# Sigmoid gates of the merge in seven block products, two whole gates ahead of the attention's last transposes; the last up projection likewise

## The chip, the core and the metric

The kernel runs on one core of one Trainium2 chip. The time is device microseconds (us) for one execution of the whole program, all weights streamed from HBM in fp32. Engines are named as in the profile: PE (TensorE matmul) and PEld (its weight load), DVE (VectorE), ACT (ScalarE), POOL (GpSimd) and SP, whose queue issues all weight loads.

## The reference, cut to what matters

Two transformer blocks run one after the other. The first has two layers ("a0", "a1"). The second has two layers too ("b0", "b1"), and the change is in those. There, layer 0 works on 512 tokens (256 of x and 256 of a context), layer 1 on the 256 tokens of x alone.

```python
def merge_branches(o_mla, o_gqa, o_four, gate_cols, lp):
    g_mla, g_gqa, g_four = jnp.split(jax.nn.sigmoid(gate_cols), N_BRANCH, axis=-1)
    y = (g_mla * (o_mla @ lp["w_br_mla"])
         + g_gqa * (o_gqa @ lp["w_br_gqa"])
         + g_four * (o_four @ lp["w_four"]))
    return y @ lp["w_o"]

def conv_ffn_2(h, lp):
    u = h @ lp["w_up"]                       # 1024 -> 2 x 2816
    u = depthwise_conv_width_3(u) + lp["conv_b"]
    a, v = jnp.split(u, 2, axis=-1)
    return (jax.nn.silu(a) * v) @ lp["w_down"]
```

The gate columns are `h @ w_in[:, 1952:]`, 3 x 1024 columns with an inner length of 1024.

## The kernel before, in words

Activations stand feature-major: 128 features on the partitions, tokens along the free axis. A matmul of the program has a 128x128 weight tile as its stationary side and 256 or 512 tokens as its moving side; the trace has two MATMUL records for each. Weight tiles come in the order of use as slabs. There are two slots for slabs (`slots`), and a slab is asked for by SP as soon as the slab before the last is used up (`static_slab`, `load`).

**The merge** (stage `merge{l}`, from L2437). There are 8 output tiles m and 3 branches b, 24 steps. A step is a gate (8 matmuls, `tensor_gate`, L2455) and a branch (4 matmuls, L2471). ACT forms the sigmoid (L2484), DVE the product with the branch (L2491), POOL adds the branches up in `Y` (L2500). A slab holds the 36 tiles of one m. The first gate stands inside the attention: `tensor_pairs` calls `late` after the transposes of the last unit but one, `tensor_gate_first`.

**Seven block products.** The up projection of b0 (`SEVEN`) is done in another way. Its weights for one m, gate half and value half, are taken as a 2x2 matrix of blocks (half by inner half), and the tokens as a 2x2 matrix (inner half by token half). The product of two such matrices needs seven block products in place of eight, in the form of Winograd. A block product is 4 matmuls (`product`, L858). POOL forms the sums s1 and s3 of weight blocks, DVE s2 and s4 (L947, L949), before PE uses them, and DVE forms four token sums t1 to t4 once per projection. Afterwards DVE combines the products: u2, u3, c22, c21 (L1000 to L1010) and c12 (L991); ACT copies p1 out of PSUM (L929). Block 0 is done whole (L840), while the sums for block 1 are formed. The order on PE within a block is p1, p6, p7, p5, p4, a12 (added to p1), p3.

**The up projection of b1** is done plainly (`tensor_up`, L660): per m 16 matmuls with 256 columns, then bias and scale on ACT (L729), four convolution taps on DVE (L754), silu on ACT (L732), the product on POOL (L781). Both forms run as a loop of 4 pairs or blocks a turn, with the rest written out.

The order of work on each engine is the program's order; nothing reorders it. Waits are on counting semaphores that each engine's own instructions raise.

## Time and profile before

| | us |
|---|---|
| median of 3 runs | 2697.74 |
| lowest and highest | 2694.82 and 2699.82 |
| the profiled execution | 2699.97 |
| its span, first to last instruction | 2697.9 |
| PE busy in the span | 2626.1 |

The mean granted clock of PE in the profiled execution is 0.979 of full speed. The profile's page gives totals; the timeline gives groups of like instructions with their start and their extent. Neighbouring groups of PE overlap a little, because the drain of one matmul lies beside the next, so a group's price is the distance from its start to the next group's start.

### The profile page before, as it was taken

What the parts mean: (1) busy time and instruction counts of PE and PEld (TensorE: products, weight loads), DVE (VectorE), ACT (ScalarE), POOL (GpSimd) and SP (SyncE); (2) the same over time, 40 slices, a digit from 0 to 9 for tenths busy, and PEclk for the clock granted to TensorE, in tenths of its full rate; (3) what the DMA queues carried; (4) which work ended last, traced back from release to release, by engine and by line L of the source; (5) the groups of instructions that cost most, each with busy time, mean ns of one, the idle gap of its engine ahead of it and who ended that gap; (6) DMA issues with size and microseconds to landing.
All of it is one profiled execution on the core that took longest, in us unless ns stands there. A gap on an engine that the chain in (4) does not pass through costs nothing.

```text
span 2697.9 us, 28700 instructions
## 1 busy us (share of the span) xinstructions
PE 2626.1 (97%) x11142; PEld 1942.6 (72%) x11142; DVE 934.2 (35%) x1793; ACT 534.5 (20%) x1075; POOL 350.9 (13%) x322
## 2 busy tenths in 40 slices
PE   7999999999899999999999999999999999999999
PEld 5756888886577888744654446888846865887887
DVE  3024167741313868313620003554401235102220
ACT  1122132111212221112530001222100124102320
POOL 0011111000101111001420001233200004100100
PEclk9989999999899999999999999999999998999999
DMA  5422377733234776121001112122311220233342
GB/s 201 154 94 78 110 281 275 288 138 143 91 124 167 270 268 245 63 95 40 1 36 70 70 66 94 63 93 93 118 47 70 94 103 1 106 143 134 146 174 102
DMA packets 31394, 333.84 MB, mean 124 GB/s; under 512 B 2880, under 2 KB 9152, under 8 KB 9152
## 3 DMA queue, kind: packets, MB, share of 16 engines
q1 hardware_dynamic: 31296, 332.45, 32.7%
q8 instruction: 72, 1.18, 0.2%
q14 instruction: 26, 0.21, 0.0%
HBM read 331.39 MB, written 1.05 MB: 123 GB/s over the span
## 4 chain that ended last, share of the span: by engine, by line
PE 95%; DVE 3%; POOL 1%; ACT 1%; issue 1%; DMA 0%; DVEq 0%; POOLq 0%; ACTq 0%
PE PS L552 26%; PE PS L660 17%; PE PS L858 9%; PE PS L2455 9%; PE PS L1414 5%; PE PS L1572 5%; PE PS L2471 5%; PE PS L1232 3%; PE PS L1584 2%; PE PS L2052 2%; PE PS L1255 2%; PE PS L1243 2%; PE PS L430 1%; PE PS L2168 1%; PE PS L2324 1%; PE PS L1084 1%
## 5 line engine op out<-in xcount | busy, mean ns | idle before, releaser
L660 PE MATMUL PS<-XN,slot 128*128 128x256 f32 x2112 | 461.3, 382 | 10.0 <-DVE XN L492 5.1
L660 PEld LDWEIGHTS PS<-XN,slot 128*128 128x128 f32 x2112 | 404.4, 192 | 66.9 <-issue 11.1
L552 PE MATMUL PS<-arena,slot 128*128 128x256 f32 x1824 | 400.9, 382 | 9.7 <-POOL arena L1973 5.4
L552 PEld LDWEIGHTS PS<-arena,slot 128*128 128x128 f32 x1824 | 349.5, 192 | 60.2 <-POOL arena L1973 6.5
L552 PE MATMUL PS<-XN,slot 128*128 128x256 f32 (+1 forms) x1248 | 312.4, 411 | 5.0 <-DVE XN L492 5.0
L552 PEld LDWEIGHTS PS<-XN,slot 128*128 128x128 f32 x1248 | 237.8, 191 | 76.7 <-issue 43.0
L2455 PE MATMUL PS<-XN,slot 128*128 128x512 f32 (+1 forms) x768 | 255.5, 486 | 0.0
L2455 PEld LDWEIGHTS PS<-XN,slot 128*128 128x128 f32 x768 | 145.8, 190 | 101.2 <-issue 91.4
L754 DVE SCALAR_TENSOR_TENSOR arena<-PS,small,arena 128x255 f32<-128x255 f32 (+1 forms) x264 | 108.8, 473 | 201.4 <-ACT arena L729 201.4
L1572 PE MATMUL PS<-arena,slot 128*128 128x512 f32 x328 | 141.1, 592 | 0.0
L610 DVE CUSTOM_DVE_ANT_1 arena<-arena 128x1024 f32<-128x1024 f32 x96 | 136.7, 1424 | 0.0
L1373 POOL TENSOR_SCALAR probs<-probs,pair_rec 128x512 f32<-128x512 f32 (+2 forms) x64 | 88.2, 1383 | 263.8 <-DVE pair_rec L1341 263.8
L440 ACT ACTIVATE SQ<-X 128x512 f32<-128x512 f32 x56 | 34.1, 628 | 439.8 <-DVE X L1526 228.2
L610 DVE CUSTOM_DVE_ANT_1 PS<-arena 128x1024 f32<-128x1024 f32 x96 | 118.5, 1235 | 0.0
L1572 PEld LDWEIGHTS PS<-arena,slot 128*128 128x128 f32 x328 | 62.3, 190 | 78.0 <-issue 78.0
L781 POOL TENSOR_TENSOR arena<-arena 128x256 f32 (+1 forms) x66 | 59.5, 901 | 451.0 <-ACT arena L732 451.0
L858 PE MATMUL PS<-SQ,slot 128*128 128x256 f32 x496 | 112.3, 379 | 0.0
L858 PEld LDWEIGHTS PS<-SQ,slot 128*128 128x128 f32 x496 | 94.2, 190 | 12.8
L1414 PE MATMUL PS<-slot,XN 128*128 128x512 f32 (+1 forms) x320 | 100.9, 475 | 2.6 <-DVE SQ L1919 2.6
L474 POOL TENSOR_TENSOR SQ<-SQ 128x512 f32<-128x512 f32 x30 | 41.1, 1374 | 436.5 <-ACT SQ L440 435.9
L2491 DVE TENSOR_TENSOR probs<-probs,PS 128x512 f32<-128x512 f32 (+1 forms) x32 | 17.8, 555 | 228.2 <-PE PS L2471 153.8
L858 PE MATMUL PS<-XN,slot 128*128 128x256 f32 x416 | 95.0, 379 | 0.0
(229 smaller groups left out, 2783.9 us busy)
## 6 DMA issues: line engine op xcount, KB each, us to landing
slot<-in_weights SPq DMA_DIRECT2D x86, 2048.0 KB, 7.7
arena<-in_mod SPq DMA_DIRECT2D x48, 1024.0 KB, 7.3
slot<-in_weights SPq DMA_DIRECT2D x16, 2816.0 KB, 9.8
slot<-in_weights SPq DMA_DIRECT2D x16, 2304.0 KB, 8.6
slot<-in_weights SPq DMA_DIRECT2D x2, 2176.0 KB, 8.5
slot<-in_weights SPq DMA_DIRECT2D x4, 1024.0 KB, 4.8
small<-in_small SPq DMA_DIRECT2D x1, 2685.0 KB, 19.2
arena<-in_c SPq DMA_DIRECT2D x2, 1024.0 KB, 10.4
```

The lines of the kernel that those rows point to most:

```text
L552: mm = pe.matmul(o, l, r, start=k == 0, stop=k == len(terms) - 1, skip_group_check=True)
L610: op = dve.tensor_tensor_reduce(w if g else MODP, w, MODC[:, g, :, :], 1.0, 0.0, ALU.mult, ALU.add, total)
L660: mm = pe.matmul(o, slots[slot][:, a:a + P], XN[:, k, seg[g]], start=k == 0, stop=k == DK - 1, skip_group_check=True)
L754: op = dve.scalar_tensor_tensor(out=o, in0=shifted(ps[:, half, :], lo + d, hi + d), scalar=conv_col(s, m, half, c), in1=o, op0=ALU.mult, o ...
L781: pool.tensor_tensor(dst, hb[:, 0, :], hb[:, 1, :], ALU.mult).then_inc(*tick(GD, s, "h", p))
L858: mm = pe.matmul(PS[:, bank, 0:T], lhs[:, k * P:(k + 1) * P], rhs[:, k, :], start=first and k == 0, stop=last and k == 3, skip_group_check ...
L1232: mm = pe.matmul(PS[:, 2 * (u % 2) + i, c0:c1], lhs, rhs, start=a, stop=z, skip_group_check=True)
L1373: op = pool.tensor_scalar(pr, pr, pair_rec[:, u % RING, j:j + 1], None, ALU.mult)
L1414: mm = pe.matmul(PS[:, bank, 0:cols_n], lhs(k, t), r, start=k == 0, stop=k == k_tiles - 1)
L1572: mm = pe.matmul(PS[:, m % 4, :], next_tiles(pe), rhs(k, slice(0, 2 * T)), start=k == 0, stop=k == k_tiles - 1, skip_group_check=True)
L2455: mm = pe.matmul(gate_ps(u), next_tiles(pe), XN[:, k, 0:nq], start=k == 0, stop=k == DK - 1, skip_group_check=True)
L2471: mm = pe.matmul(branch_ps(u), next_tiles(pe), BR[b][:, k, 0:nq], start=k == 0, stop=k == 3, skip_group_check=True)
```

## The change

`SEVEN` now holds b1 as well, and all functions of that form (`tensor_up_seven`, `scalar_up_seven`, `vector_up_seven`, `gpsimd_up_seven`) take the segments; with 256 tokens a block product has 128 columns. On DVE the weight sums of the next block move from the front of a block to a place behind the third combination.

The merge is cut into 12 steps, 4 pairs of output tiles (t) by 3 branches. A step has one slab of 24 tiles: 16 of the two gates, 8 of the two branches. In a step after the first the two gates are one seven-product block; the first step does both whole (`gate_whole`), and both stand where one gate stood, in front of the last transposes. The sums s1, s2, s4 of the weights stand in the free part of the slot, the token sums in the arena (`TM`).

```diff
-SEVEN = ("b0",)
+SEVEN = ("b0", "b1")
...
-        for m in range(8):
-            slab = []
+        for t in range(4):
             for b, name in enumerate((f"w_br_mla_2{l}", f"w_br_gqa_2{l}", f"w_four_2{l}")):
-                slab += down_tiles(w, DK, [m], col=1952 + b * D) + down_tiles(name, 4, [m])
-            merge.append(slab)
+                g0, g1 = [down_tiles(w, DK, [2 * t + i], col=1952 + b * D) for i in range(2)]
+                merge.append(g0[0::2] + g0[1::2] + g1[0::2] + g1[1::2]
+                             + down_tiles(name, 4, [2 * t, 2 * t + 1]))
...
-            def tensor_gate_first(pe, gate=tensor_gate):
+            def tensor_gate_first(pe, gate=gate_whole, slot_of=merge_slot):
+                _, sem, landed = slot_of(0)
+                pe.wait_ge(sem, landed)
                 gate(pe, 0)
+                gate(pe, 1)
...
+                for u, (t, b) in enumerate(steps):
+                    slot, sem, landed = slot_of(u)
                     if u:
-                        gate(pe, u)
+                        a11, a12, s3, a22 = quarters(slot)
+                        s1, s2, s4 = sums(slot)
+                        pe.wait_ge(sem, landed)
+                        pe.wait_ge(*of(s, "sig", 2 * u - 2))
+                        product(a11, XQ[:, :, 0, 0:hq], BA, last=False).then_inc(*tick(TD, s, "p1", u))
+                        pe.wait_ge(*of(s, "sums", u))
+                        if u == 1:
+                            pe.wait_ge(*of(s, "t4"))
...
+                        else:
+                            pe.wait_ge(*of(s, "u2", u - 1))
+                        product(s2, TM[:, 1], BB).then_inc(*tick(TD, s, "p6", u))
...
+                        product(s3, TM[:, 2], BC).then_inc(*tick(TD, s, "p7", u))
+                        pe.wait_ge(*(of(s, "c12", u - 1) if u > 1 else of(s, "sig", 1)))
+                        product(s1, TM[:, 0], BD, last=False).then_inc(*tick(TD, s, "p5", u))
...
+                        product(a22, TM[:, 3], BE).then_inc(*tick(TD, s, "p4", u))
+                        pe.wait_ge(*of(s, "p1_copied", u))
+                        product(a12, XQ[:, :, 1, 0:hq], BA, first=False)
+                        pe.wait_ge(*of(s, "c22", u))
+                        product(s4, XQ[:, :, 1, hq:nq], BD, first=False).then_inc(*tick(TD, s, "p3", u))
...
+            def vector_merge(dve, s=s, l=l, nq=nq, hq=hq, fu=fu, n_units=len(units), slot_of=merge_slot,
+                             quarters=merge_quarters, sums=merge_sums, TM=TM):
...
+                    if u < len(steps) - 1:
+                        a11, a12, _, _ = quarters(slot_of(u + 1)[0])
+                        s1, s2, s4 = sums(slot_of(u + 1)[0])
+                        dve.wait_ge(*of(s, "s3", u + 1))
+                        dve.tensor_tensor(s2, s1, a11, ALU.subtract).then_inc(*tick(VD, s, "s2", u + 1))
+                        dve.wait_ge(*of(s, "s2", u + 1))
+                        dve.tensor_tensor(s4, a12, s2, ALU.subtract).then_inc(*tick(VD, s, "sums", u + 1))
...
+            def gpsimd_merge(pool, s=s, nq=nq, slot_of=merge_slot, quarters=merge_quarters, sums=merge_sums):
+                for u, (t, b) in enumerate(steps):
+                    if u < len(steps) - 1:
+                        slot, sem, landed = slot_of(u + 1)
+                        a11, _, a21, a22 = quarters(slot)
+                        pool.wait_ge(sem, landed)
+                        pool.tensor_tensor(sums(slot)[0], a21, a22, ALU.add).then_inc(*tick(GD, s, "s1", u + 1))
+                        pool.tensor_tensor(a21, a11, a21, ALU.subtract).then_inc(*tick(GD, s, "s3", u + 1))
```

In `vector_up_seven` the order within a block changes (abridged; h is half the tokens):

```diff
                     .then_inc(*w_tick(s, VD, "c12", i, turn))
+                tap_steps(i, turn, m)
                 if turn is None and i == FM:
-                    tap_steps(i, turn, m)
                     return
...
-                if turn is not None or i < FM - 1:
-                    weight_sums(i, turn)
-                dve.wait_ge(*w_of(s, "p6", i, turn))
-                dve.wait_ge(*w_of(s, "p1_copied", i, turn))
-                dve.tensor_tensor(U2, PS[:, 4, 0:T], P1C, ALU.add).then_inc(*w_tick(s, VD, "u2", i, turn))
-                tap_steps(i, turn, m)
```

The three places on which the order matters, as it stands in the two programs. In these rows `xN` counts matmuls of the program, L2455 is a gate of before, L2465 (`gate_whole`) the whole gates of after, L2481 (`product`) a product of the merge, L2471 and L2520 branches, L1232 and L1236 scores, L1243 and L1247 transposes, L1255 and L1259 values.

PE, from the last transposes but one of the attention of layer 0 into the merge, before:

```order
L1243 MATMUL PS<-small,probs 128x128 x8
L2455 MATMUL PS<-XN,slot1 128x512 x8
L1255 MATMUL PS<-rms,arena 64x128 x8
L1243 MATMUL PS<-small,probs 128x128 x8
L1255 MATMUL PS<-probs_t,arena 64x128 x8
L1255 MATMUL PS<-rms,arena 64x256 x4
L2471 MATMUL PS<-arena,slot1 128x512 x4
L2455 MATMUL PS<-XN,slot1 128x512 x8
```

and now:

```order
L1247 MATMUL PS<-small,probs 128x128 x8
L2465 MATMUL PS<-XN,slot1 128x512 x16
L1259 MATMUL PS<-rms,arena 64x128 x8
L1247 MATMUL PS<-small,probs 128x128 x8
L1259 MATMUL PS<-probs_t,arena 64x128 x8
L1259 MATMUL PS<-rms,arena 64x256 x4
L2520 MATMUL PS<-arena,slot1 128x512 x8
L2481 MATMUL PS<-XN,slot0 128x256 x4
L2481 MATMUL PS<-arena,slot0 128x256 x16
L2481 MATMUL PS<-XN,slot0 128x256 x8
L2520 MATMUL PS<-arena,slot0 128x512 x8
```

The second gate has moved up in front of the last value groups and transposes; behind the two branches of step 0 the next block stands in the other slot.

DVE, in the merge of layer 1 of before (gated products alone, L2491):

```order
L1358 COPY probs_t<-PS 128x512
L1358 COPY rms<-PS 128x512
L2491 TENSOR_TENSOR arena<-probs,PS 128x256
L2491 TENSOR_TENSOR probs<-probs,PS 128x256 x2
L2491 TENSOR_TENSOR arena<-probs,PS 128x256
```

and now, where L1362 is the same copy, L2561 to L2566 are the token sums, L2593 and L2595 the weight sums s2 and s4, L2571 to L2587 the combinations u2, u3, c22, c21, c12 and L2601 the gated products:

```order
L1362 COPY probs_t<-PS 128x512
L1362 COPY rms<-PS 128x512
L2561 TENSOR_TENSOR arena<-XN 128x4x128
L2562 TENSOR_TENSOR arena<-XN 128x4x128
L2564 TENSOR_TENSOR arena<-XN,arena 128x4x128
L2566 TENSOR_TENSOR arena<-arena,XN 128x4x128
L2593 TENSOR_TENSOR slot0<-slot0 128x512
L2595 TENSOR_TENSOR slot0<-slot0 128x512
L2601 TENSOR_TENSOR arena<-probs,PS 128x256 x2
L2571 TENSOR_TENSOR arena<-PS,arena 128x128
L2575 TENSOR_TENSOR arena<-PS,arena 128x128
L2581 TENSOR_TENSOR arena<-PS,arena 128x128
```

The sums stand between the attention's last copy and the first gated products; from then on each step has its five combinations ahead of the weight sums of the next slab.

DVE, in the up projection of layer 1: before, a pair had the four taps alone (L754, each 128x255). One block now, from those written out behind the loop (L995 is c12, L980 the taps, L1002 to L1008 u2, u3 and c22, L951 and L953 the weight sums):

```order
L995 TENSOR_TENSOR PS<-PS,arena 128x128
L980 SCALAR_TENSOR_TENSOR arena<-arena,small 128x255
L980 SCALAR_TENSOR_TENSOR arena<-PS,small,arena 128x255
L980 SCALAR_TENSOR_TENSOR arena<-arena,small 128x255
L980 SCALAR_TENSOR_TENSOR arena<-PS,small,arena 128x255
L1002 TENSOR_TENSOR arena<-PS,arena 128x128
L1005 TENSOR_TENSOR arena<-PS,arena 128x128
L1008 TENSOR_TENSOR arena<-PS,arena 128x128
L951 TENSOR_TENSOR probs<-probs,slot 128x512
L953 TENSOR_TENSOR probs<-slot,probs 128x512
L1013 TENSOR_TENSOR arena<-arena,PS 128x128
```

Seven operations have come to the four taps, and the weight sums stand behind three of the five combinations.

## Rows read from the trace of the kernel before

**Rows 1.** The page: engine totals, and the chain that ended last by engine.

```profile
PE 2626.1 (97%) x11142; PEld 1942.6 (72%) x11142; DVE 934.2 (35%) x1793; ACT 534.5 (20%) x1075; POOL 350.9 (13%) x322
...
PE 95%; DVE 3%; POOL 1%; ACT 1%; issue 1%; DMA 0%; DVEq 0%; POOLq 0%; ACTq 0%
```

**Rows 2.** Timeline of PE, merge of layer 0: start us, us, engine line op tiles xcount.

```profile
1382.50 7.03 PE L2455 MATMUL PS<-XN,slot 128*128 128x512 f32 x16
1389.36 3.60 PE L2471 MATMUL PS<-arena,slot 128*128 128x512 f32 x8
```

**Rows 3.** Timeline of PE, merge of layer 1.

```profile
2383.95 3.62 PE L2455 MATMUL PS<-XN,slot 128*128 128x256 f32 x16
2387.40 1.89 PE L2471 MATMUL PS<-arena,slot 128*128 128x256 f32 x8
2389.13 3.62 PE L2455 MATMUL PS<-XN,slot 128*128 128x256 f32 x16
```

**Rows 4.** Timeline of PE, up projection of layer 0, same place of two neighbouring turns.

```profile
1730.45 7.07 PE L858 MATMUL PS<-SQ,slot 128*128 128x256 f32 x32
...
1754.62 7.07 PE L858 MATMUL PS<-SQ,slot 128*128 128x256 f32 x32
```

**Rows 5.** Timeline of PE, up projection of layer 1.

```profile
2460.77 155.01 PE L660 MATMUL PS<-XN,slot 128*128 128x256 f32 x704 [4.83 <-ACT XN L454]
```

**Rows 6.** Timeline of PE, value tokens of layer 1: 128-column products, and what follows.

```profile
2129.35 7.31 PE L1414 MATMUL PS<-slot,XN 128*128 128x128 f32 x64
2136.49 7.07 PE L552 MATMUL PS<-XN,slot 128*128 128x256 f32 x32
```

**Rows 7.** Timeline of PE, end of the attention of layer 1.

```profile
2296.92 3.62 PE L2455 MATMUL PS<-XN,slot 128*128 128x256 f32 x16
2300.47 1.09 PE L1255 MATMUL PS<-rms,arena 128*64 128x128 f32 x16
2301.50 1.09 PE L1243 MATMUL PS<-small,probs 128*128 128x128 f32 x8
2302.52 1.09 PE L1255 MATMUL PS<-probs_t,arena 128*64 128x128 f32 x16
```

**Rows 8.** Timeline of POOL and DVE, weight sums in the up projection of layer 0.

```profile
1741.05 1.27 POOL L1026 TENSOR_TENSOR slot<-slot 128x512 f32<-128x512 f32 x1 [3.05 <-PE PS L858]
...
1743.58 0.69 DVE L947 TENSOR_TENSOR slot<-slot 128x512 f32<-128x512 f32 x1 [2.14 <-POOL slot L1027]
1744.31 0.69 DVE L949 TENSOR_TENSOR slot<-slot 128x512 f32<-128x512 f32 x1
```

**Rows 9.** DMA issues of weights in four stretches: count, KB each, us to landing.

```profile
slot<-in_weights SPq DMA_DIRECT2D x1, 1024.0 KB, 4.7
...
slot<-in_weights SPq DMA_DIRECT2D x9, 2048.0 KB, 8.5
...
slot<-in_weights SPq DMA_DIRECT2D x6, 2304.0 KB, 8.7
...
slot<-in_weights SPq DMA_DIRECT2D x9, 2048.0 KB, 7.4
```

**Rows 10.** Timeline of ACT and DVE, up projection of layer 1.

```profile
2540.12 1.02 ACT L729 ACTIVATE arena<-PS,small 128x256 f32<-128x256 f32 x2 [3.61 <-PE PS L660]
2541.32 1.65 DVE L754 SCALAR_TENSOR_TENSOR arena<-PS,small,arena 128x255 f32<-128x255 f32 x4 [5.25 <-ACT arena L729]
```

**Rows 11.** Timeline of DVE, combining step of a block, up projection of layer 0.

```profile
1748.42 0.42 DVE L1007 TENSOR_TENSOR arena<-PS,arena 128x256 f32<-128x256 f32 x1
```

**Rows 12.** Timeline of POOL and of DVE where they overlap, up projection of a0.

```profile
407.68 1.08 POOL L781 TENSOR_TENSOR arena<-arena 128x256 f32 x1 [5.58 <-ACT arena L732]
414.35 0.73 POOL L781 TENSOR_TENSOR arena<-arena 128x256 f32 x1 [5.58 <-ACT arena L732]
...
408.11 1.74 DVE L610 CUSTOM_DVE_ANT_1 arena<-arena 128x1024 f32<-128x1024 f32 x1
...
410.92 1.21 DVE L610 CUSTOM_DVE_ANT_1 arena<-arena 128x1024 f32<-128x1024 f32 x1
```

More of the change, by code:

```diff
@@ L832, in first @@
                 claim(pe, 7)
-                for g in range(2):
+                for g in segs:
                     for half in range(2):
@@ L857, in product @@
                     for k in range(4):
-                        mm = pe.matmul(PS[:, bank, 0:T], lhs[:, k * P:(k + 1) * P], rhs[:, k, :], start=first and k == 0,
+                        mm = pe.matmul(PS[:, bank, 0:h], lhs[:, k * P:(k + 1) * P], rhs[:, k, :], start=first and k == 0,
                                        stop=last and k == 3, skip_group_check=True)
@@ L866, in body @@
                     pe.wait_ge(*w_of(s, "conv", i, turn, 1))
-                product(a11, XQ[:, :, 0, 0:T], odd, last=False).then_inc(*w_tick(s, TD, "p1", i, turn))
+                product(a11, XQ[:, :, 0, 0:h], odd, last=False).then_inc(*w_tick(s, TD, "p1", i, turn))
+                pe.wait_ge(*w_of(s, "sums", i, turn, 1))
                 if start:
-                    pe.wait_ge(*of(s, "sums", "block", 0))
                     pe.wait_ge(*of(s, "t2"))
@@ L2451, in tensor_gate, with merge_slot @@
-            def tensor_gate(pe, u, s=s, nq=nq, banks_of=banks_of, gate_ps=gate_ps):
-                for bank in set(banks_of(u)):
-                    claim(pe, bank)
+            g_merge = first_slab[s]
+            hq = nq // 2
+            TM = area(4096, 16 * T).rearrange("p (s k t) -> p s k t", s=4, t=T)
+            BA, BD, BB, BC, BE, BBR = 0, 1, 2, 3, 4, 5
+            def merge_slot(u, g_merge=g_merge):
+                g = g_merge + u
+                return slots[g % 2], sems[f"landed{g % 2}"], 16 * (g // 2 + 1)
@@ L2456, in tensor_gate @@
                                    skip_group_check=True)
[L2457 to L2459 removed]
+                mm.then_inc(*tick(TD, s, "gate", i))
+            def tensor_gate_first(pe, gate=gate_whole, slot_of=merge_slot):
+                _, sem, landed = slot_of(0)
+                pe.wait_ge(sem, landed)
                 gate(pe, 0)
[L2462 to L2475 removed]
@@ L2477, in scalar_merge @@
-            def scalar_merge(act, s=s, l=l, nq=nq, gate_ps=gate_ps, wide=wide, n_units=len(units)):
-                act.wait_ge(*of(f"batt{l}", "turned", n_units - 1, 0))
-                for u in range(len(steps)):
-                    act.wait_ge(*of(s, "gate" if wide else "branch", u))
-                    if u >= 3:
-                        act.wait_ge(*of(s, "sum" if (u - 3) % 3 else "gated", u - 3))
-                    act.activation(GT[:, u % 3, 0:nq], gate_ps(u), ACT.Sigmoid).then_inc(*tick(SD, s, "sig", u))
@@ new lines, in scalar_merge, with sigmoid @@
+            def scalar_merge(act, s=s, l=l, nq=nq, hq=hq, n_units=len(units)):
+                act.wait_ge(*of(f"batt{l}", "turned", n_units - 1, 0))
+                def sigmoid(j, src):
+                    if j >= 4:
+                        act.wait_ge(*of(s, "sum" if steps[j // 2 - 2][1] else "gated", j - 4))
+                    act.activation(GT[:, j % 4, 0:nq], src, ACT.Sigmoid).then_inc(*tick(SD, s, "sig", j))
+                for i in range(2):
+                    act.wait_ge(*of(s, "gate", i))
+                    sigmoid(i, PS[:, i, 0:nq])
+                for u in range(1, len(steps)):
+                    act.wait_ge(*of(s, "p1", u))
+                    if u > 1:
+                        act.wait_ge(*of(s, "u2", u - 1))
+                    act.activation(P1C[:, 0:hq], PS[:, BA, 0:hq], ACT.Copy).then_inc(*tick(SD, s, "p1_copied", u))
+                    act.wait_ge(*of(s, "c21", u))
+                    sigmoid(2 * u + 1, CU[:, 0:nq])
+                    act.wait_ge(*of(s, "c12", u))
+                    sigmoid(2 * u, PS[:, BA, 0:nq])
```

211 lines of the change are left out of this document (138 added, 73 removed).

## Prediction, written before the changed kernel ran

> **What bounds the kernel now.** I read the page's chain first: 95% of what ended last is PE, none of it DMA [rows 1], and PE is busy for 2626.1 of 2697.9 us. So work taken from PE is worth its full price, as long as no other engine becomes the one PE waits for. I then read the timeline of PE in the three stages that change, for the start-to-start distance of neighbouring groups, since durations overlap. Every matmul of the program is two MATMUL records. With 512 columns, 16 records (one gate) take 1389.36 - 1382.50 = 6.86 us [rows 2]. With 256 columns 16 records take 2387.40 - 2383.95 = 3.45 us, 0.2156 us each, and the 8 of a branch 1.73 [rows 3]. A seven-product block at 256 columns is 56 records; two of them take 1754.62 - 1730.45 = 24.17 us, 12.09 each, with PE never idle [rows 4]. The up projection of layer 1 is 704 records, 22 pairs of 32, after a gap of 4.83 us that the change leaves alone [rows 5].
>
> **What a 128-column product costs.** In layer 1 the products have 128 columns, and no product of this kind exists before. The nearest rows are the value tokens: 64 records of the same full 128x128 weights, each with its own load, in 2136.49 - 2129.35 = 7.14 us, 0.1116 each [rows 6]. The other row of that width is the transposes at the end of the attention, 8 in 2302.52 - 2301.50 = 1.02 us, 0.1275 each [rows 7]. I take 0.1116: same kind of operation, weights and k loop, while a transpose is another operation with waits between its groups. A block is then 56 x 0.1116 = 6.25 us.
>
> **The savings on PE.** One pair of gates, or of up halves, gives up 32 records and takes 56 narrower ones.
> - Merge of layer 0: 2 x 6.86 - 12.09 = 1.63 us, 11 blocks: 18.0 us. The first pair stays whole.
> - Merge of layer 1: 2 x 3.45 - 6.25 = 0.65 us, 11 blocks: 7.2 us.
> - Up projection of layer 1: 32 x 0.2156 - 6.25 = 0.65 us, 21 blocks: 13.7 us. Block 0 stays whole.
> Together 38.9 us. The branches cost what they did.
>
> **What is moved.** The second whole gate goes in front of the last transposes. PE does not idle there now [rows 7], so the move gains nothing; it delays the last turn by one gate, 6.86 or 3.45 us, and everything on DVE behind it. Behind the last turn DVE must copy it, form four token sums and two weight sums, before the second product of block 1. Sized by the DVE rows of 512 elements, 0.69 each [rows 8], that is seven operations, 4.9 us in layer 1; PE meanwhile has two values groups of 1.02 [rows 7], two branches of 1.73 [rows 3] and a first product of 0.89: 6.4 us. In layer 0 PE's cover doubles and the token sums do too. I cost it at nothing; without cover it would be at most a few us, once per layer. The end of the merge keeps its cover: the last sum is used only by the output projection's eighth matmul.
>
> **The new chain in the merge.** Each step now has its own slab of 24 tiles, 1536 KB, and there are two slots. The slab of step u+1 is asked for when step u-1 ends. It must land, then POOL forms two sums and DVE two more; from POOL's start to DVE's end this took 1745.00 - 1741.05 = 3.95 us [rows 8]. PE needs them after all of step u and one product: 6.25 + 3.45 + 0.89 = 10.6 us in layer 1. 1536 KB is not in the trace. Between 1024 KB in 4.7 and 2304 KB in 8.7 [rows 9] a line gives 6.3 us; from the quicker 2048 KB (7.4) it is 6.05, from the slower (8.5) 7.15. With 0.6 us for the hand-overs (estimate) the sums stand at 0.6 + 6.3 + 3.95 = 10.85: 0.25 late. A late step moves the next request back as well, so only every second step pays: 5 x 0.25 = 1.3 us. The ends are 0 and 5 x 1.1 = 5.5 us. In layer 0 a step is 12.09 + 6.86 = 19 us, and nothing is late. I take 1.3.
>
> **The chain in the up projection of layer 1.** DVE has four taps, 1.65 us [rows 10], two weight sums, 1.38, and five small combinations. One of 256 elements takes 0.42 [rows 11], one of 512 0.69, so 128 is about 0.28: 1.4 us together. That is 4.45 us of work in a block of 6.25. In the new order (combination, taps, three combinations, weight sums, last combination) I follow it from the block's start: taps wait for ACT and end at 2.4, the third combination waits for PE's fourth product and ends at 4.05, the sums end at 5.5, the last at 5.75. PE wants the third combination at 5.36 and the sums at 6.25 + 0.89 = 7.14. POOL's two sums start at 0.25 and end at 2.8. Where a new slab is needed, the request is one block older and lands 7.4 to 8.5 us after it [rows 9], which puts the sums at most 0.5 us before they are wanted. Everything fits, so I cost it at nothing; but cover is down to about a microsecond. Moving the weight sums behind the taps touches layer 0 too, where a block is 12.09 us and hides it.
>
> Contention is the doubt. Before, DVE waits while POOL forms its sums; now it runs taps that read SBUF twice. Where the two overlap in a0, a POOL operation of 0.73 takes 1.08 and a DVE one of 1.21 takes 1.74 [rows 12], so about 0.5 us on DVE per overlap. Two overlaps bring DVE to about 5.5 us of work and its chain to 6.2 to 6.7: level with PE's 6.25. The Trainium skill (SBUF — State Buffer, "SBUF: two separate sides") says that the port pair of DVE and GpSimd is an exclusive lock, held for a whole instruction, also against a DVE operation with two SBUF inputs; by that, two taps would each wait out a POOL sum, DVE's chain would come out near 6.55 and the sum would be the one of rival A.
>
> **The sum.** 38.9 - 1.3 = 37.6 us. The profiled execution took 2699.97 us, 2.2 above the median of 2697.74. So 2699.97 - 37.6 = 2662.4 for such an execution and 2660.2 against the median; I say 2661.
>
> **Rivals.**
> A. DVE and POOL set the pace of the up projection, and the merge's loads land at the slow end. Blocks of 6.55 instead of 6.25 cost 21 x 0.3 = 6.3 us, the merge 5.5: 38.9 - 11.8 = 27.1, so 2697.7 - 27.1 = 2671. For it: the rows on overlap and a cover of only a microsecond. Against: most of POOL's work lies beside taps of which two read PSUM.
> B. 128-column products run at the transposes' 0.1275. A block is 7.14, 0.89 more in 32 blocks: 28.5 us lost, 9 us left: 2689. For it: only that row, which has waits inside.
> C. The slower one: the weight load binds. 128-column products pay for 75% more loads; if a load does not hide behind 128 columns, a record costs between 0.1116 and 0.2156 (the 256-column one). The whole change turns slower where 56 d exceeds 6.90 + 18.0 / 32 = 7.46, at d = 0.133 us. At the middle, 0.16, a block is 8.96: 32 x 2.06 - 18.0 = 48 us slower, 2746. Against it stand the value tokens, whose loads are the same. The Trainium skill (TensorE: Matmul & The Clock Gate, "Back-to-back issue gap") says so of bf16: at N=128 a stream of loads and matmuls runs at about 81 ns against 56 for the matmul alone. By that ratio on half a 256-column record d would be 0.157 (estimate), a block 8.8 us, the time about 2740; the row disagrees.
> D. The order of waits hides a stall that I do not see, such as ACT late with a copy that a product waits for, and takes back most of the gain: 2685 to 2697.
>
> **Chances.** Forecast 0.63, A 0.25, B 0.04, C 0.04, D 0.04. The range for eight in ten takes the forecast and A with their bounds: from no stall at all (2659) less a few us between chips to A's end with a few more: 2655 to 2676. A measurement tells about 0.2%, 5.4 us, from no change; faster than 2692.3 are the forecast, A, B and most of D: 0.94. Same 0.02, slower 0.04.
>
> **What the profile will show.** Right: blocks of 12.09 us in the merge of layer 0 and about 6.25 in layer 1; 8 records of a product in 0.89; PE idle in every second step of merge 1 by some tenths, its releaser a DVE sum; no idle PE inside the up projection of layer 1; DVE busy some 75 to 85% there. Wrong: a record at 128 columns over 0.12 (B, C); PE idle in each block before the weight-sum or s4 product (A); PE idle at block 1 of a merge (the moved gate).

## The result, and the profile after

The changed kernel takes 2665.97 us (median of four executions, 2662.73 to 2668.98) against 2696.58 for the kernel before (2694.82 to 2699.82): ratio 0.9885, 95% interval 0.9869 to 0.9901, 30.6 us faster. The forecast said 2661 with a range of 2655 to 2676. The profiled execution took 2663.59 us, its span is 2661.8.

The page of the changed kernel: busy time, share of the span and instructions of each engine, and the chain that ended last by engine. It answers to [rows 1].

```profile
PE 2583.7 (97%) x12174; PEld 1996.3 (75%) x12174; DVE 1109.5 (42%) x2106; ACT 534.0 (20%) x1109; POOL 469.8 (18%) x408
...
PE 91%; DVE 4%; issue 2%; POOL 1%; DMA 1%; ACT 1%; DVEq 0%; ACTq 0%; POOLq 0%
```

PE is busy 42 us less and still for 97% of the span, though its share of the last chain has fallen from 95 to 91%: DVE, issue and DMA have a point more each. DVE has 175 us more work, POOL 119 us more.

The timeline of PE in the merge of layer 0, changed kernel (start us, us, engine line op tiles xcount), for [rows 2]:

```profile
1387.75 1.89 PE L2481 MATMUL PS<-XN,slot 128*128 128x256 f32 x8
1389.47 7.07 PE L2481 MATMUL PS<-arena,slot 128*128 128x256 f32 x32
1396.38 3.62 PE L2481 MATMUL PS<-XN,slot 128*128 128x256 f32 x16
1399.83 7.03 PE L2520 MATMUL PS<-arena,slot 128*128 128x512 f32 x16
1406.70 1.89 PE L2481 MATMUL PS<-XN,slot 128*128 128x256 f32 x8
```

A step is the seven products (8 + 32 + 16 records, 1399.83 - 1387.75 = 12.08 us) and the two branches (1406.70 - 1399.83 = 6.87), with no idle time in brackets: the predicted 12.09 and 6.86.

The same in the merge of layer 1, two steps, for [rows 3]:

```profile
2285.41 1.05 PE L2481 MATMUL PS<-XN,slot 128*128 128x128 f32 x8
2286.31 3.74 PE L2481 MATMUL PS<-arena,slot 128*128 128x128 f32 x32
2289.88 1.95 PE L2481 MATMUL PS<-XN,slot 128*128 128x128 f32 x16
2291.67 3.62 PE L2520 MATMUL PS<-arena,slot 128*128 128x256 f32 x16
2295.12 1.05 PE L2481 MATMUL PS<-XN,slot 128*128 128x128 f32 x8
2296.99 3.84 PE L2481 MATMUL PS<-arena,slot 128*128 128x128 f32 x32 [0.82 <-DVE slot L2595]
...
2305.91 1.05 PE L2481 MATMUL PS<-XN,slot 128*128 128x128 f32 x8
```

32 records of 128 columns take 2289.88 - 2286.31 = 3.57 us, 0.1116 each, the value tokens' price [rows 6]. The first step is 2295.12 - 2285.41 = 9.71 us (6.26 for the products, 3.45 for the branches). The second is 10.79: the product of s2 waits for DVE's last weight sum (L2595). Timeline of POOL and DVE ahead of that wait, and the DMA issue that answers to [rows 9] (x, KB, us from issue to landing), of that step and of the merge:

```profile
2293.00 1.26 POOL L2610 TENSOR_TENSOR slot<-slot 128x512 f32<-128x512 f32 x1 [17.83 <-DMA slot<-in_weights]
...
2296.25 0.69 DVE L2595 TENSOR_TENSOR slot<-slot 128x512 f32<-128x512 f32 x1
...
slot<-in_weights SPq DMA_DIRECT2D x1, 1536.0 KB, 7.3
...
slot<-in_weights SPq DMA_DIRECT2D x10, 1536.0 KB, 6.7
```

The slab is asked for at 2285.61, POOL starts when it has landed, 7.4 us later, and DVE ends at 2296.94. Of the eleven steps four take 9.71 us and seven are longer, by 1.08, 0.99, 0.09, 0.25, 0.42, 1.25 and 0.45 us, in sum 4.5. The three largest stand in steps whose slab took 7.2 to 7.9 us to land. At first every second step is late; further on four late ones follow one another.

And the up projection of layer 1, an odd block, for [rows 5]:

```profile
2494.88 1.06 PE L860 MATMUL PS<-SQ,probs 128*128 128x128 f32 x8
...
2498.45 1.06 PE L860 MATMUL PS<-XN,slot 128*128 128x128 f32 x8
2499.92 1.16 PE L860 MATMUL PS<-XN,probs 128*128 128x128 f32 x8 [0.41 <-DVE arena L1008]
2500.91 1.06 PE L860 MATMUL PS<-XN,slot 128*128 128x128 f32 x8
```

The last product, of s4, waits for the third combination (DVE L1008). Eight blocks in this part of the stretch (2474.02 to 2527.87) take 53.85 us, so two take about 13.45 where 2 x 6.25 = 12.5 was expected. The last four blocks are back at about 6.25.

By stages, from the start of the first row of a stretch to the start of the stretch behind it, each from the kernel's own trace. The late gate is the first whole gate, the one that stands inside the attention:

| us | before | before, second trace | changed | changed, second trace |
|---|---|---|---|---|
| to the late gate of merge 0 | 1368.03 | 1363.15 | 1362.99 | 1362.82 |
| merge 0 from its late gate | 251.36 | 251.36 | 233.24 | 233.25 |
| from there to the late gate of merge 1 | 677.53 | 677.54 | 674.68 | 674.67 |
| merge 1 from its late gate | 128.47 | 128.47 | 125.84 | 126.30 |
| up projection, layer 1 | 154.85 | 154.86 | 147.32 | 142.89 |

(The second traces come from the experiments.) The changed stretches give 18.1, 2.2 to 2.6 and 7.5 to 12.0 us.

### The profile page after: what moved, and what is told of

The parts are those of the page before. It is cut to its first block, busy times and chain, and to the rows that moved or that the text cites. A ratio compares the mean times of both kernels' runs of the same rounds, so it can differ in the third digit from the quotient of the medians.

```text
span 2661.8 us, 31643 instructions
## 1 busy us (share of the span) xinstructions
PE 2583.7 (97%) x12174; PEld 1996.3 (75%) x12174; DVE 1109.5 (42%) x2106; ACT 534.0 (20%) x1109; POOL 469.8 (18%) x408
## 4 chain that ended last, share of the span: by engine, by line
PE 91%; DVE 4%; issue 2%; POOL 1%; DMA 1%; ACT 1%; DVEq 0%; ACTq 0%; POOLq 0%
PE PS L552 26%; PE PS L860 12%; PE PS L660 12%; PE PS L2481 7%; PE PS L1577 5%; PE PS L1418 5%; PE PS L2520 4%; PE PS L1236 3%; PE PS L1589 2%; PE PS L2057 2%; PE PS L1247 2%; PE PS L1259 2%; PE PS L430 1%; PE PS L842 1%; PE PS L2173 1%
## 5 line engine op out<-in xcount | busy, mean ns | idle before, releaser
L552 PEld LDWEIGHTS PS<-arena,slot 128*128 128x128 f32 x1824 | 348.8, 191 | 60.0 <-POOL arena L1978 6.6
L552 PE MATMUL PS<-XN,slot 128*128 128x256 f32 (+1 forms) x1248 | 312.4, 411 | 5.0 <-DVE XN L492 5.0
L660 PE MATMUL PS<-XN,slot 128*128 128x256 f32 x1408 | 306.3, 381 | 5.1 <-DVE XN L492 5.1
L660 PEld LDWEIGHTS PS<-XN,slot 128*128 128x128 f32 x1408 | 268.7, 191 | 42.8 <-issue 5.9
L552 PEld LDWEIGHTS PS<-XN,slot 128*128 128x128 f32 x1248 | 237.8, 191 | 76.7 <-issue 43.0
L860 PE MATMUL PS<-SQ,slot 128*128 128x256 f32 (+1 forms) x992 | 172.9, 327 | 0.0
L860 PEld LDWEIGHTS PS<-SQ,slot 128*128 128x128 f32 x992 | 152.2, 191 | 12.8
L860 PE MATMUL PS<-XN,slot 128*128 128x256 f32 (+1 forms) x832 | 148.1, 328 | 0.0
L860 PEld LDWEIGHTS PS<-XN,slot 128*128 128x128 f32 x832 | 128.7, 191 | 11.7
L2481 PE MATMUL PS<-arena,slot 128*128 128x256 f32 (+1 forms) x704 | 119.6, 328 | 2.9 <-DVE slot L2595 2.9
L1577 PEld LDWEIGHTS PS<-arena,slot 128*128 128x128 f32 x328 | 62.3, 190 | 78.0 <-issue 78.0
L2481 PEld LDWEIGHTS PS<-arena,slot 128*128 128x128 f32 x704 | 107.0, 191 | 13.1 <-DVE slot L2595 4.0
L754 DVE SCALAR_TENSOR_TENSOR arena<-PS,small,arena 128x254 f32<-128x254 f32 (+1 forms) x176 | 72.4, 471 | 82.1 <-ACT arena L729 82.1
L980 DVE SCALAR_TENSOR_TENSOR arena<-arena,small 128x510 f32<-128x510 f32 (+1 forms) x84 | 91.8, 1093 | 14.2 <-ACT arena L925 14.2
```

The lines of the kernel that those rows point to most:

```text
L552: mm = pe.matmul(o, l, r, start=k == 0, stop=k == len(terms) - 1, skip_group_check=True)
L660: mm = pe.matmul(o, slots[slot][:, a:a + P], XN[:, k, seg[g]], start=k == 0, stop=k == DK - 1, skip_group_check=True)
L754: op = dve.scalar_tensor_tensor(out=o, in0=shifted(ps[:, half, :], lo + d, hi + d), scalar=conv_col(s, m, half, c), in1=o, op0=ALU.mult, o ...
L860: mm = pe.matmul(PS[:, bank, 0:h], lhs[:, k * P:(k + 1) * P], rhs[:, k, :], start=first and k == 0, stop=last and k == 3, skip_group_check ...
L980: op = dve.scalar_tensor_tensor(out=o[:, :, lo:hi], in0=x[:, :, lo + d:hi + d], scalar=conv_col(s, m - 1, half, c), in1=o[:, :, lo:hi], op ...
L1577: mm = pe.matmul(PS[:, m % 4, :], next_tiles(pe), rhs(k, slice(0, 2 * T)), start=k == 0, stop=k == k_tiles - 1, skip_group_check=True)
```

## The experiments

**The theories.** For the up projection of layer 1, theory P: DVE's taps on the combined half have two SBUF inputs and stand behind POOL's weight sums, so the third combination is late. Theory L: the chain of ACT, taps and combinations is too long by itself. Theory B: POOL slows DVE whatever it reads. For the merge of layer 1, theory M: the sums are late because the slab lands late, and nothing else is lost; theory N: a loss that would show up at the next wait.

The profile speaks for P before any run. Timeline of DVE and of POOL, changed kernel, the same odd block:

```profile
2495.76 1.27 DVE L980 SCALAR_TENSOR_TENSOR arena<-arena,small 128x255 f32<-128x255 f32 x1 [0.81 <-ACT arena L925]
2496.95 0.47 DVE L980 SCALAR_TENSOR_TENSOR arena<-PS,small,arena 128x255 f32<-128x255 f32 x1
2497.35 1.09 DVE L980 SCALAR_TENSOR_TENSOR arena<-arena,small 128x255 f32<-128x255 f32 x1
2498.36 0.47 DVE L980 SCALAR_TENSOR_TENSOR arena<-PS,small,arena 128x255 f32<-128x255 f32 x1
...
2499.57 0.29 DVE L1008 TENSOR_TENSOR arena<-PS,arena 128x128 f32<-128x128 f32 x1
...
2495.49 1.26 POOL L1030 TENSOR_TENSOR slot<-slot 128x512 f32<-128x512 f32 x1 [2.22 <-DMA slot<-in_weights]
2496.71 1.44 POOL L1031 TENSOR_TENSOR slot<-slot 128x512 f32<-128x512 f32 x1
```

The tap at 2496.95, which reads PS, takes 0.47 us in the middle of a POOL operation. The two that read arena for both inputs take 1.27 and 1.09, and each ends 0.28 to 0.29 us after a POOL operation does (2497.03 against 2496.75; 2498.44 against 2498.15). So they look held until POOL is done.

### The changed kernel again

No edit.

> The changed kernel once more, beside the next three on one chip. Expected 2663 to 2669 us, 30 us under the kernel before; the stretches as in its first profile: up projection of layer 1 147.3 us, merge of layer 1 125.8 us (from its late gate to the first matmul of the output projection). What differs from profile to profile by more than 0.3 us in stretches that the edit does not touch is noise of the granted clock.

Measured: 2664.37 us (2659.42 to 2668.72), ratio to before 0.9886 (0.9869 to 0.9902). The stretches are in the table above. One of them did not repeat: the up projection took 142.89 us, 4.4 less. It is not the noise of the granted clock that I had expected such differences to be: over the seven-product blocks the clock was 1.00 in both traces. Timeline of DVE in an odd block of this trace:

```profile
2507.26 0.48 DVE L980 SCALAR_TENSOR_TENSOR arena<-arena,small 128x255 f32<-128x255 f32 x1 [0.72 <-ACT arena L925]
2507.68 0.48 DVE L980 SCALAR_TENSOR_TENSOR arena<-PS,small,arena 128x255 f32<-128x255 f32 x1
2508.08 1.07 DVE L980 SCALAR_TENSOR_TENSOR arena<-arena,small 128x255 f32<-128x255 f32 x1
...
2507.58 1.29 POOL L1030 TENSOR_TENSOR slot<-slot 128x512 f32<-128x512 f32 x1 [2.82 <-DMA slot<-in_weights]
```

Here the first tap starts 0.32 us before POOL's first sum and takes 0.48; only the second meets POOL. In the first trace the tap starts 0.27 us after POOL and takes 1.27. A few tenths of a microsecond decide it. A late tap makes DVE late for the next block, which would explain why a stretch stays one way for many blocks; the run that holds POOL back, below, bears on that.

The place where the two traces part can be seen. The slab asked for at 2460.96 took 8.8 us to land here; the same slab, asked for at 2460.90, took 7.5 in the first trace. So POOL's sums came after DVE's taps for once, the weight sums were late, and PE waited for them (this trace, the only long wait in the stretch):

```profile
2475.56 3.83 PE L860 MATMUL PS<-SQ,slot 128*128 128x128 f32 x32 [1.17 <-DVE slot L953]
```

The ten blocks from 2481.02 to 2543.55 then take 6.25 us each, so here a slower load led into the quicker way. That is one trace and no test: the run with the later product of s2, below, has a slab of 8.8 us and a wait of 1.24 at the same place, its blocks take 6.25 us before it and for four more behind it, and then it falls into the slow way.

### The combined half in PSUM

In `vector_up_seven` and `w_sources`; bank 7 is lent again when the last block's taps are done.

```diff
+            cu = PS[:, 7, 0:n] if n == T else CU
...
-                dve.tensor_tensor(CU[:, h:n], PS[:, 2 + i % 2, 0:h], U3[:, 0:h], ALU.add)
+                dve.tensor_tensor(cu[:, h:n], PS[:, 2 + i % 2, 0:h], U3[:, 0:h], ALU.add)
...
-                dve.tensor_tensor(CU[:, 0:h], U3[:, 0:h], PS[:, 6, 0:h], ALU.subtract)
+                dve.tensor_tensor(cu[:, 0:h], U3[:, 0:h], PS[:, 6, 0:h], ALU.subtract)
...
-            return [PS[:, (i - 1) % 2, 0:n], PS[:, 7, 0:n] if first else CU[:, 0:n]]
+            return [PS[:, (i - 1) % 2, 0:n], PS[:, 7, 0:n] if first or n == T else CU[:, 0:n]]
```

> In the up projection of layer 1 alone, the combined half that DVE and ACT read from SBUF is put into the free PSUM bank 7, so that no tap reads SBUF with both inputs. Theory P (the taps with two SBUF inputs stand behind POOL's weight sums, so DVE's third combination is late for PE's last product): taps of this half fall from 1.09-1.40 us to 0.47 beside POOL, PE's idle time before the s4 product goes, blocks come to 6.25 us, the stretch from 147.3 to about 141.2 us, the kernel 6 us faster than the changed one (2660). Theory L (the chain ACT, four taps, three combinations with 0.8 and 0.4 us between them is too long by itself): taps get shorter but PE still idles about 0.4 us in every second block, and the stretch stays above 145 us. Theory B (POOL slows DVE whatever it reads): the taps stay above 1 us, no change.

Measured: 2659.10 us (2657.34 to 2659.84), ratio 0.9859 (0.9842 to 0.9875); the stretch 140.87 us. Groups of DVE in this stretch, this kernel and then the changed one (line engine op names shapes xcount | busy us, mean ns | idle before us):

```profile
L982 DVE SCALAR_TENSOR_TENSOR arena<-PS,small,arena 128x255 f32<-128x255 f32 x81 | 34.9, 479 | 13.7 <-ACT arena L926 13.5
```

```profile
L980 DVE SCALAR_TENSOR_TENSOR arena<-arena,small 128x255 f32<-128x255 f32 x38 | 37.2, 978 | 13.7 <-ACT arena L925 13.7
L980 DVE SCALAR_TENSOR_TENSOR arena<-PS,small,arena 128x255 f32<-128x255 f32 x41 | 19.2, 473 | 4.5 <-ACT arena L925 4.5
```

All taps now take 0.48 us, though POOL's sums are as long as before (1.27), and PE idles nowhere behind the 4.83 us at the start of the stretch. P holds; L and B fall. The four times also lie within 2.5 us of each other, where the changed kernel's lay 6.3 and 9.3 apart. The taps are not the only DVE operation that is held: the first of its two weight sums (128x512, all in SBUF), with POOL's product beside it (0.72), takes 0.97 to 1.20 us in place of 0.69 in most blocks, in the changed kernel and in this one alike. Here that costs nothing, because it stands behind the third combination.

### POOL's sums cut

```diff
+                if s == "b1":
+                    s1, a11, a21, a22 = [ap[:, 0:8] for ap in (s1, a11, a21, a22)]
                 pool.tensor_tensor(s1, a21, a22, ALU.add).then_inc(*w_tick(s, GD, "s1", i, turn))
```

> In the up projection of layer 1 POOL's two weight sums are cut to 8 of 512 columns (the part left out); all waits stay. Theories P and B: without a long POOL operation beside them the taps take 0.47 us, blocks 6.25 us, the stretch about 141.2 us against 147.3. Theory L: the stretch stays above 145 us. Together with the run before: if both reach 141, it is the two SBUF inputs beside POOL; if only this one does, it is POOL's work or its lateness, not what the taps read.

The kernel leaves out 504 of the 512 columns of each of POOL's two sums.

Measured: 2660.07 us (2658.68 to 2664.83), ratio 0.9869 (0.9853 to 0.9885); the stretch 140.92 us. Taking the work from POOL and taking the second SBUF input from the taps give the same 6.4 us. Removing either one is enough, so the cause is the two together.

### POOL held back

```diff
                 if turn is not None or i > 0:
                     pool.wait_ge(*w_of(s, "p3", i, turn, 1))
+                    if s == "b1":
+                        pool.wait_ge(*w_of(s, "tap1", i, turn))
```

> In the up projection of layer 1 POOL starts its two weight sums only once DVE's first tap is done; nothing is left out and nothing moved to PSUM. Theory R (there are two ways for the stretch to run: with DVE's first tap ahead of POOL's first sum, as mostly in the second profile, 142.9 us, or behind it, as in the first, 147.3 us, and a late tap keeps the next one late): the first tap now always takes 0.48 us, only the second of that half meets a POOL sum, the third combination is ready at about 4.9 us of the block against 5.4 wanted, the stretch is 141 to 142 us in this profile and the times lie within some 3 us of each other, near 2660.5. The rival: what is held back makes the weight sums late for the s2 product, or delays DVE's round by more than it has to spare; then TensorE waits there in each block, and the stretch is over 145 us.

Measured: 2662.78 us (2660.27 to 2664.81), ratio 0.9877 (0.9860 to 0.9893); the stretch 143.25 us, between the two expectations. Timeline of DVE in two neighbouring blocks:

```profile
2495.01 0.48 DVE L980 SCALAR_TENSOR_TENSOR arena<-arena,small 128x255 f32<-128x255 f32 x1 [0.81 <-ACT arena L925]
...
2495.84 1.29 DVE L980 SCALAR_TENSOR_TENSOR arena<-arena,small 128x255 f32<-128x255 f32 x1
...
2501.46 0.48 DVE L980 SCALAR_TENSOR_TENSOR arena<-arena,small 128x255 f32<-128x255 f32 x1 [0.84 <-ACT arena L925]
```

The first tap takes 0.48 or 0.49 in every block, and the second one that reads SBUF twice 1.24 to 1.51 in all but two. But DVE's round is 2501.46 - 2495.01 = 6.45 us, over PE's 6.25, with only 0.3 us of idle time in it beside the 0.84 in which it waits for ACT's bias. So one held tap in a block already makes DVE the pace, by 0.2 us; with two in every second block and one in the others the round was 13.45 / 2 = 6.7. Theory R is half right: the first tap is always short, and this stretch is within 0.4 us of the quicker of the two ways, but the times spread over 4.5 us where it said some 3.

### The weight sums ahead of the taps

In the up projection of layer 1 alone, the order of before; in short:

```diff
                     .then_inc(*w_tick(s, VD, "c12", i, turn))
-                tap_steps(i, turn, m)
+                weight_sums(i, turn)
                 dve.wait_ge(*w_of(s, "p6", i, turn))
                 dve.wait_ge(*w_of(s, "p1_copied", i, turn))
                 dve.tensor_tensor(U2[:, 0:h], PS[:, 4, 0:h], P1C[:, 0:h], ALU.add)
+                tap_steps(i, turn, m)
...
-                weight_sums(i, turn)
                 dve.wait_ge(*w_of(s, "p4", i, turn))
```

> In the up projection of layer 1 alone, DVE's order of before: weight sums and first small combination ahead of the taps. The taps then run behind POOL's sums and not beside them, which frees them of contention, but they wait for them. Worked from durations: POOL's sums end 2.8 us into the block, DVE's two at 4.2, first combination 4.5, four taps 6.3, third combination 7.1, where TensorE wants it at 5.4: blocks of about 8.0 us, the stretch about 178 us, the kernel some 31 us slower than the changed one, near 2697. If instead the contention were worth more than the waiting, the stretch would fall below 147 us.

Measured: 2690.61 us (2687.47 to 2695.93), ratio 0.9982 (0.9973 to 0.9991); the stretch 169.99 us. Timeline of PE and of DVE:

```profile
2507.14 0.69 DVE L951 TENSOR_TENSOR slot<-slot 128x512 f32<-128x512 f32 x1 [2.29 <-POOL slot L1037]
...
2508.68 0.47 DVE L980 SCALAR_TENSOR_TENSOR arena<-arena,small 128x255 f32<-128x255 f32 x1
...
2511.00 1.16 PE L860 MATMUL PS<-XN,probs 128*128 128x128 f32 x8 [1.13 <-DVE arena L1014]
```

DVE waits 2.29 us for POOL's sums; behind them the taps take 0.47 each, so nothing contends with them, and the s4 product still waits 1.1 to 1.3 us in nearly every block. A block is (169.99 - 9.65) / 21 = 7.64 us (9.65 is the first block, done whole, in the changed kernel's trace, 2441.79 - 2432.14), where I had expected 8.0. Moving the weight sums behind the taps, which cost nothing in layer 0 (its whole up projection takes 267.63 us before and 267.64 after), is what makes the seven products pay in layer 1: without it their 7.5 us turn into a loss of 15.

### The up projection in pairs

```diff
-SEVEN = ("b0", "b1")
+SEVEN = ("b0",)
```

> One part of the change undone: the up projection of layer 1 in pairs of halves with 256 columns as before, the merges as changed. By the traces this stretch returns to 154.9 us, 7.5 us over the changed kernel's first profile and 12.0 over its second, so 2672 to 2676 us; the merge stretches stay at 233.2 and 125.8 us. If the merges' gain leaned on the up projection (or the reverse), the time is outside 2668 to 2680.

Measured: 2673.03 us (2671.08 to 2678.78), ratio 0.9914 (0.9901 to 0.9928); the stretch 154.13 us, the merges 233.25 and 126.98. The parts are separate: this one is worth 7.1 us by the changed kernel's first median and 8.7 by its second, of some 31.

### The product of s2 later in the merge

In the merge of layer 1 alone, from step 2 on, in short (the waits for banks move with their products):

```diff
                         product(a11, XQ[:, :, 0, 0:hq], BA, last=False).then_inc(*tick(TD, s, "p1", u))
-                        product(s2, TM[:, 1], BB).then_inc(*tick(TD, s, "p6", u))
+                        pe.wait_ge(*of(s, "s3", u))
                         product(s3, TM[:, 2], BC).then_inc(*tick(TD, s, "p7", u))
                         product(s1, TM[:, 0], BD, last=False).then_inc(*tick(TD, s, "p5", u))
+                        pe.wait_ge(*of(s, "sums", u))
+                        product(s2, TM[:, 1], BB).then_inc(*tick(TD, s, "p6", u))
```

> In the merge of layer 1 alone, TensorE takes the products of s3 and s1, which need only POOL's sums, ahead of the product of s2, which needs DVE's. Theory M (the slab lands some 7 us after it is asked for, so the sums are up to 1 us late in every second step, and nothing else is lost): the sums are wanted 1.8 us later, the idle time of 0.2 to 1.0 us before the s2 product goes, the stretch falls from 125.8 to about 121.5 us, the kernel by 4.3 us. Theory N (the loss would come back at the next wait: the s2 product is now third of the three that the combinations need, and the third combination becomes late for the last product): idle time moves to the s4 product, and the stretch stays above 124.5 us.

Measured: 2659.83 us (2655.17 to 2666.90), ratio 0.9867 (0.9845 to 0.9888); the merge of layer 1 121.74 us. Of the 4.6 us lost against 128.47 - 7.2 = 121.3, 4.1 come back. M holds: the loss was the lateness of DVE's sums, by up to about a microsecond, and it does not reappear at the next wait. One idle time of 0.23 us is left before an s2 product. The up projection took 146.31 us in this trace, untouched by the edit and between its two ways to run, which is why the whole times spread.

### The second gate behind the last transposes

```diff
                 gate(pe, 0)
-                gate(pe, 1)
...
                 assert Stream.slab == g_merge and Stream.tile == 0
+                gate(pe, 1)
```

> In both merges only the first whole gate stands ahead of the attention's last transposes, the second behind them, where the changed kernel has both ahead. My prediction costed the place at nothing: the stretches from the first gate to the output projection stay at 233.2 and 125.8 us within 0.3. The rival: in front, the second gate delays the last turn and DVE's token sums behind it, or behind, it closes cover that the values need; then the place shows as idle PE at the last transposes or before the first s2 product, 0.5 to 3.5 us per layer.

Measured: 2664.47 us (2662.86 to 2666.75), ratio 0.9878 (0.9863 to 0.9893), the same as the changed kernel. The stretches: 233.25 and 126.63 us, the latter 0.3 over the changed kernel's second trace and 0.8 over its first. Timeline of PE, this kernel, merge of layer 0:

```profile
1365.26 7.03 PE L2465 MATMUL PS<-XN,slot 128*128 128x512 f32 x16
1372.22 1.09 PE L1259 MATMUL PS<-rms,arena 128*64 128x128 f32 x16
...
1376.18 7.13 PE L2465 MATMUL PS<-XN,slot 128*128 128x512 f32 x16
```

No idle time on either side. In layer 0 the place is worth nothing. In layer 1 the difference is no larger than what the landing of slabs moves from trace to trace (125.84 to 126.98 over kernels that are alike there), so it shows nothing either.

### The kernel before again

> The kernel before, profiled a second time. In the two first profiles 7.9 us of the difference lie outside the stretches that the change touches (5.0 us up to the first gate of merge 0, 2.9 between the feed-forward block of layer 0 and merge 1). If those are chance, a second trace of before has its first gate of merge 0 nearer to 1363 to 1365 us, where all changed kernels have it, or the 2.9 us gone; if they come from the change, both repeat. The touched stretches repeat within 0.7 us: 251.4, 128.5 and 154.9.

Measured: one execution, 2695.11 us. The late gate of merge 0 starts at 1363.15, as in all the changed kernels (1362.8 to 1365.5): the 5.0 us were chance (1362.8 to 1368.0 over all traces). In the first trace of before the value tokens at 217.40 took 8.59 us for 16 records that take 7.03 elsewhere. The 2.9 us repeat: 677.54 against 674.67 to 674.69 in all traces with the change. They come from the granted clock at the same work. Windows of 3 us (busy time of PE, PEld, DVE, ACT, POOL, then granted clock, DMA share, GB/s), kernel before and then changed kernel, counted from the same PE row:

```profile
2214.00:2217.00 3.00, 3.00 (x7) 1.41 (x7) 2.22 (x5) 0.00 (x0) 0.00 (x0) 0.50 0.00 0
2217.00:2220.00 3.00, 3.00 (x11) 1.66 (x10) 1.28 (x3) 0.00 (x0) 2.27 (x4) 0.50 0.00 0
2220.00:2223.00 3.00, 3.00 (x8) 1.18 (x4) 2.04 (x4) 0.00 (x0) 1.58 (x4) 0.50 0.00 0
```

```profile
2190.90:2193.90 3.00, 3.00 (x9) 1.63 (x8) 2.46 (x6) 0.00 (x0) 0.26 (x1) 0.65 0.00 0
2193.90:2196.90 3.00, 3.00 (x13) 1.46 (x12) 1.94 (x5) 0.00 (x0) 2.78 (x5) 0.78 0.00 0
2196.90:2199.90 3.00, 3.00 (x13) 1.56 (x11) 2.79 (x7) 0.00 (x0) 2.74 (x5) 0.79 0.02 5
```

Before, PE stands at 0.50 (1.2 GHz) throughout; after, it is granted more in these windows, and counted from that row it is back at 1.00 (2.4 GHz) for good some 2 us earlier. PE's rows ahead of this place have the same spacing in both kernels. Why the clock is granted differently here is not settled by any run.

### Both edits

The PSUM half and the later product of s2 together.

> Both edits together: in the up projection of layer 1 the combined half in PSUM, in the merge of layer 1 the s3 and s1 products ahead of the s2 product. If the two losses are separate, their stretches are 140.9 and 121.7 us as in the runs that had one edit each, and the kernel takes 2659.1 - 4.5 = 2654.6 us. If one loss only hid the other, or the gains came from where the runs happened to stand, it stays at 2658 or more.

Measured: 2651.96 us (2651.51 to 2653.17 in five executions), ratio 0.9834 (0.9821 to 0.9848): it is faster than both kernels, 14.0 us under the changed one. The stretches are 121.67 and 139.73 us, so the two losses are separate. Timeline of PE, merge of layer 1, for the same step as above:

```profile
2295.30 1.05 PE L2483 MATMUL PS<-XN,slot 128*128 128x128 f32 x8
2296.19 3.74 PE L2483 MATMUL PS<-arena,slot 128*128 128x128 f32 x32
...
2305.00 1.05 PE L2483 MATMUL PS<-XN,slot 128*128 128x128 f32 x8
```

9.70 us, no wait. The time is also 2.6 us under the 2654.6 expected. Part of that shows in the traces: up to the late gate of merge 0 this trace is 2.3 us shorter than the one with the PSUM edit alone (1363.16 against 1365.48), which is chance as above; and the up projection is 1.1 us under it, in its first, whole block (8.52 against 9.72 us for its 32 records), which follows 4.83 us of idle PE. Windows of 2 us that begin 1 and 3 us after PE has started on that block, this kernel and then the changed one:

```profile
2429.10:2431.10 2.00, 2.00 (x7) 1.60 (x6) 1.97 (x5) 1.68 (x5) 0.00 (x0) 0.54 0.00 0
2431.10:2433.10 2.00, 2.00 (x11) 1.77 (x10) 2.00 (x4) 0.00 (x0) 0.00 (x0) 1.00 0.00 0
```

```profile
2433.10:2435.10 2.00, 2.00 (x6) 1.62 (x5) 1.97 (x5) 1.69 (x5) 0.00 (x0) 0.50 0.03 8
2435.10:2437.10 2.00, 2.00 (x6) 1.55 (x6) 2.00 (x4) 0.00 (x0) 0.00 (x0) 0.50 0.00 0
```

After the same idle time the clock is back at full (1.00, 2.4 GHz) 3 us into the block in the first, and at 0.50 (1.2 GHz) in the second.

## Why the prediction was right or wrong

- **The price of a 128-column product**: right. 0.1116 us per record in both stages that use it; rivals B and C are out. The rule of the Trainium skill on streams of loads and 128-column matmuls (TensorE: Matmul & The Clock Gate, "Back-to-back issue gap"), scaled as I had scaled it, gave an estimate of 0.157; these fp32 products do not show it.
- **Merge of layer 0**: right, 18.1 us for 18.0.
- **The moved gate, and the first pair in front**: right, nothing.
- **The merge's load chain**: right in mechanism, the term mis-sized: 4.5 us for 1.3. I had put the sums at 10.85 us from the end of a step, 0.25 late, in every second step; seven of the eleven steps were late. In the first late step they were ready at 2296.94 - 2285.41 = 11.5. POOL and DVE took 2296.94 - 2293.00 = 3.94, as costed; it is the load that took 7.3 from issue to landing, where I had interpolated 6.3 (the median of the merge's loads is 6.7). With that median and the hand-overs as measured (0.2 us up to the request, 0.1 behind the landing) the chain is 0.2 + 6.7 + 0.1 + 3.94 = 10.9, about what I had costed. So the spread was what I left out: the three steps whose slabs took 7.2 to 7.9 us lost 3.3 of the 4.5. Also, a wait costs more than its idle time in brackets: 0.82 idle made the step 1.08 longer.
- **The chain of the up projection in layer 1**: wrong. The step that failed is "Everything fits, so I cost it at nothing". I had the third combination ready at 4.05 us of the block; it was ready 5.9 us into the block shown above (its row at 2499.57 ends at 2499.86, the block began 0.89 before the PE row at 2494.88), against 5.36 wanted. Three things add up. The taps start late: 1.77 us into the block (2495.76 - 2493.99) where I had 0.75, because DVE comes late from its previous round. The four taps take 1.35 more (2498.76, where the next operation starts, less 2495.76 is 3.0, in place of 1.65). The three small combinations take 0.25 more, since they start 0.40 apart when each waits for the one before, and not 0.28. Together 2.6 us, of which 0.8 was cover, as I had DVE waiting that long for PE's fourth product; 1.8 is left. I had costed an overlap with POOL at 0.5 us; the held taps lost 0.8 and 0.6. The stretch saved 7.5 us (first trace) or 12.0 (second), not 13.7. With the lock gone it saved 154.85 - 140.87 = 14.0, so the saving on PE was right and the cover was not.
- **Rival A**: it named the cause and, for the up projection, the size. It said blocks of 6.55 us and 5.5 us for the merge; the first trace has (147.32 - 9.65) / 21 = 6.56 and 4.5. The 5.5 rests on a slip: from the slower 2048 KB load (8.5) the line that gave 6.3 gives (4.7 + 8.5) / 2 = 6.6 us for 1536 KB, and not 7.15, so the slow end was 0.55 us late and 2.8 us in sum. The loads in fact took 6.3 to 7.9, so that end coming close is luck. The weighing between forecast and rival was off: my objection was that most of POOL's work lies beside taps of which two read PSUM. That is so, and helps nothing, since the other two wait. By the exclusive lock of the Trainium skill (SBUF — State Buffer, "SBUF: two separate sides"), which I had left to the rival, the taps would wait out a POOL sum, and the traces agree: 1.27 and 1.09 us beside POOL, 0.47 with one input in PSUM. POOL's second sum, which starts while the first tap is still under way, is lengthened too, 1.27 to 1.44, which fits a lock that DVE can hold as well.
- **The total**: 18.1 + 2.6 + 7.5 on the changed stretches and 2.9 on the one between them make 31.1, and the medians differ by 30.6. Against the forecast's 37.6, 6.2 us were lost in the up projection (1.7 in the second trace) and 3.3 in the merge of layer 1, and 2.9 came from the clock, which I had not foreseen. That last part is luck: without it the time would be near 2669, closer to rival A's 2671 than to my 2661.
- **The signs in the profile**: DVE was busy for 111.3 of the 137.7 us of the 21 blocks, 81%, inside the 75 to 85% that I gave. PE's idle time before the s4 product, which I had named as the sign of rival A, is there in every second block of the slow part.

## What to carry to other kernels

Before an engine gets a second job beside another's, look at what each operation reads: by these traces a DVE operation with two SBUF inputs that starts beside a long POOL operation is to be costed at POOL's end and 0.28 us more, not at its own duration, and a free PSUM bank for one input removes the wait. Where products are taken in a free order, put those whose operands need the fewest steps first; four microseconds of waiting for late sums vanished by moving one product back by two. And where a chain has under a microsecond of cover, cost it at the loads' and the neighbours' slow end, not at their medians.

## What the runs showed of the hardware

- How POOL holds DVE up depends on the inputs. The same tap, same shape, took 0.47 us with one input in PSUM in the middle of a POOL operation, and 0.98 on average (38 taps) with both in SBUF, 1.09 and 1.27 where a POOL sum stood beside it; it ended 0.28 us after POOL did.
- The same instructions took 142.9 us in one trace and 147.3 in another, where two operations that hold each other up start within 0.3 us of one another.
- Two traces of the same code before and two or more after repeat to 0.01 us in a stretch (677.53 and 677.54; 674.67 and 674.68) and yet differ between the kernels by 2.86 us, through the granted clock, with the same PE rows ahead of it.
